# Embedding gate and projection with tokens on partitions, in a one-core decoder layer

## What is computed

```python
gate = jax.nn.sigmoid(_rms_norm(h, lw['norm_ple']) @ lw['w_ple_gate'])   # 1024 x 1024
h = h + gate * (p_l @ lw['w_ple_proj'])                                   # 256 x 1024
```

## Time and profile before

| | us |
|---|---|
| median of 3 executions | 1337.91 (1337.55 to 1339.97) |
| the profiled execution, its own time | 1336.66 |
| its span, first to last instruction | 1334.9 |
| TensorE busy (matmul) | 1252.0 |
| VectorE, ScalarE busy | 329.8, 201.0 |

### The profile page before, as it was taken

How to read it: one execution, slowest core, us unless ns; L and a number is a source line. 1 busy time by engine, 2 the same in 40 slices (tenths; PEclk the granted TensorE clock), 3 DMA queues, 4 the chain that set the end, 5 groups by cost and what they waited for, 6 DMA issues and landing times.

```text
span 1334.9 us, 15918 instructions
## 1 busy us (share of the span) xinstructions
PE 1252.0 (94%) x6170; PEld 618.2 (46%) x6170; DVE 329.8 (25%) x574; ACT 201.0 (15%) x385; POOL 19.9 (1%) x51
## 2 busy tenths in 40 slices
PE   7888798899999999999999999999999999999875
PEld 5768676343434343434434343434344343434354
DVE  7773224112111111121121111111211211111233
ACT  3423403001011010111010101101110101100022
POOL 1010000000000000000000000000000000000000
PEclk9786688899999999999999999999999999998888
DMA  8037203689999999999999999999999999998400
GB/s 254 12 128 303 76 1 135 269 360 366 401 414 405 424 406 423 389 423 408 423 403 398 403 407 423 408 422 405 422 409 423 402 415 419 399 384 368 176 2 32
DMA packets 73262, 438.47 MB, mean 328 GB/s; under 512 B 13617, under 2 KB 16817, under 8 KB 22497
## 3 DMA queue, kind: packets, MB, share of 16 engines
q1 hardware_dynamic: 72736, 437.64, 80.6%
q10 hardware_dynamic: 496, 0.43, 0.1%
HBM read 436.67 MB, written 2.41 MB: 329 GB/s over the span
## 4 chain that ended last, share of the span: by engine, by line
PE 90%; ACT 4%; DVE 3%; issue 2%; ACTq 0%; DVEq 0%
PE ps L922 39%; PE ps L939 18%; PE ps L908 10%; PE ps L878 5%; PE ps L811 2%; PE ps L1051 2%; PE ps L930 2%; PE ps L881 1%; PE ps L603 1%; PE ps L512 1%; PE ps L585 1%; PE ps L543 1%; PE ps L739 1%; PE ps L994 1%; PE ps L948 1%
## 5 line engine op out<-in xcount | busy, mean ns | idle before, releaser
L922 PE MATMUL ps<-ring_up,region 128*64 128x512 f32 x2112 | 461.9, 595 | 2.6 <-issue 1.4
L922 PEld LDWEIGHTS ps<-ring_up,region 128*64 128x64 f32 x2112 | 163.7, 137 | 282.7 <-issue 280.8
L939 PE MATMUL ps<-ring_dn,region 128*64 128x512 f32 x1056 | 246.8, 622 | 12.4 <-issue 11.0
L1825 DVE TENSOR_SCALAR region<-ps 128x512 f32<-128x512 f32 x33 | 22.8, 692 | 711.9 <-PE ps L922 711.9
L939 PEld LDWEIGHTS ps<-ring_dn,region 128*64 128x64 f32 x1056 | 82.7, 142 | 163.4 <-issue 161.2
L908 PE MATMUL ps<-region,n_tok 128*128 128x128 f32 (+1 forms) x768 | 136.7, 309 | 0.0
L908 PEld LDWEIGHTS ps<-region,n_tok 128*128 128x128 f32 (+1 forms) x768 | 105.0, 189 | 41.3 <-issue 12.4
L1304 ACT ACTIVATE region<-region 128x512 f32<-128x512 f32 x33 | 20.8, 629 | 500.3 <-DVE region L1825 500.3
L1316 ACT ACTIVATE region<-ps 64x512 f32<-64x512 f32 x66 | 39.0, 591 | 269.7 <-PE ps L939 269.3
L878 PE MATMUL ps<-region 128*128 128x512 f32 (+1 forms) x136 | 65.9, 607 | 2.6 <-issue 1.3
L922 PE MATMUL ps<-region 128*64 128x512 f32 x264 | 62.7, 592 | 0.0
(11 more groups left out here) (363 smaller groups left out, 788.6 us busy)
## 6 DMA issues: line engine op xcount, KB each, us to landing
ring_up<-in_w_up_dram SPq DMA_DIRECT2D x264, 1024.0 KB, 11.9
ring_dn<-in_w_down_dram SPq DMA_DIRECT2D x132, 1024.0 KB, 7.8
ring_dn<-in_w_out_dram SPq DMA_DIRECT2D x1, 4096.0 KB, 13.3
ring_up<-in_w_ple_gate_dram SPq DMA_DIRECT2D x4, 1024.0 KB, 6.3
ring_up<-in_w_in_dram SPq DMA_DIRECT2D x2, 1536.0 KB, 8.9
ring_up<-in_w_in_dram SPq DMA_DIRECT2D x2, 1024.0 KB, 8.9
x_tok<-in_x_prompt_dram SPq DMA_DIRECT2D x2, 512.0 KB
ring_up<-in_w_glu_dram SPq DMA_DIRECT2D x1, 1024.0 KB, 5.5
```

Source lines behind the costliest of these rows:

```text
L922: m = mm(ps[64 * (q % 2):64 * (q % 2) + 64, q // 2, :], xe[:, k, slots] if k < UP else one_hot, w, start=(k == 0), stop=(k == UP))
L939: m = mm(ps[64 * half:64 * half + 64, O_B, :], act_t[:, f % 4, 64 * (f // 4):64 * (f // 4) + 64], ring_dn[:, f, 512 * half:512 * half + 51 ...
L1825: V.tensor_scalar(g_lim, bank(0), LIMIT, None, ALU.min).then_inc(Z["g_rdy"], 1)
```

## The change

The gate and the projection are computed with tokens on partitions and 512 output columns in a piece: two halves for each of the prompt chunks and one piece for the samples, five in all. The samples' gate goes in four column groups of 256 columns, each on its own 32 partitions of PSUM; their projection goes in two groups of 512. `back` and its transposes are gone, as are the scaling and its place ahead of the transposes for the prompt chunks: the raw rows are turned as soon as the expert shares are in, and the row factor goes into the sigmoid as a scale for each partition. The samples are still scaled first. A chunk's rows are finished, normalised and stored as soon as its pieces are done, the last chunk in two halves. All five pieces of the projection now stand ahead of the counting.

```diff
-PP_BANK = (6, 7, 0, 1, 2, 6, 7, 0)
+PP_BANK = (6, 7, 0, 1, 2)
+PIECES = len(PP_BANK)
+Z_TURN = ((3, 4), (0, 1), (5, 5))
+Z_BANK = (6, 7, 2, 3, 4)
...
# SyncE
-            sp.wait_ge(Z["f_out"], 3)
-            for c in range(2):
-                sp.dma_start(O[0][0, c * P:(c + 1) * P, :], n_tok[:, c]).then_inc(Z["st_y"], 16)
+            sp.wait_ge(Z["f_out"], 1)
+            sp.dma_start(O[0][0, 0:P, :], n_tok[:, 0]).then_inc(Z["st_y"], 16)
+            sp.wait_ge(Z["f_out"], 2)
             sp.dma_start(O[1].rearrange("b l d -> (b l) d"), n_tok[0:NB, 2]).then_inc(Z["st_y"], 16)
+            for half in range(2):
+                at = slice(512 * half, 512 * half + 512)
+                sp.wait_ge(Z["f_out"], 3 + half)
+                sp.dma_start(O[0][0, P:SEQ, at], n_tok[:, 1, at]).then_inc(Z["st_y"], 16)
...
# TensorE, projection (all before the counting; the two late pieces are gone)
+            def embedding():
+                for c in range(2):
+                    for half in range(2):
+                        for k in range(2):
+                            m = mm(bank(PP_BANK[2 * c + half]), p_t[:, k, c * P:(c + 1) * P],
+                                   w_pp[:, k, 512 * half:512 * half + 512], start=(k == 0), stop=(k == 1))
+                        m.then_inc(Z["pp_ps"], 1)
+                for k in range(2):
+                    for half in range(2):
+                        m = mm(ps[64 * half:64 * half + NB, PP_BANK[4], :], p_t[:, k, SEQ:T],
+                               w_pp[:, k, 512 * half:512 * half + 512], start=(k == 0), stop=(k == 1))
+                m.then_inc(Z["pp_ps"], 1)
...
# TensorE, tail
+            def gate_rows(c, half):
+                for k in range(KD):
+                    m = mm(bank(Z_BANK[3 * c + half]), fb[:, k, c * P:(c + 1) * P], w_gate[:, k, 512 * half:512 * half + 512],
+                           start=(k == 0), stop=(k == KD - 1))
+                m.then_inc(Z["gate_ps"], 1)
+            def gate_samples():
+                for k in range(KD):
+                    for q in range(4):
+                        m = mm(ps[32 * q:32 * q + NB, Z_BANK[2], 0:256], fb[:, k, SEQ:T], w_gate[:, k, 256 * q:256 * q + 256],
+                               start=(k == 0), stop=(k == KD - 1))
+                m.then_inc(Z["gate_ps"], 1)
+            pe.wait_ge(Z["cmb_read"], (n_visits + PAIRS) * 4 + 1)
+            turn_tail(0, x_tok)
+            pe.wait_ge(Z["cmb_read"], (n_visits + PAIRS) * 4 + 4)
+            turn_tail(1, x_tok)
+            pe.wait_ge(Z["norm_sb"], 14)
+            pe.wait_ge(ld_gate_w, 64)
+            gate_rows(0, 0)
+            pe.wait_ge(Z["norm_scaled"], 7)
+            turn_tail(2, n_tok)
+            gate_rows(0, 1)
+            pe.wait_ge(Z["norm_sb"], 17)
+            gate_samples()
+            gate_rows(1, 0)
+            gate_rows(1, 1)
...
# ScalarE, tail
+            for n_, c in enumerate((0, 2, 1)):
                 act.wait_ge(Z["cmb_read"], (n_visits + PAIRS) * 4 + (1, 4, 3)[c])
+                row_square(c)
+                row_root(6 + n_ + 1, c)
+            def gate_piece(n_):
+                act.wait_ge(Z["gate_ps"], KM + n_ + 1)
+                c, half = divmod(n_, 3)
+                if n_ == 2:
+                    for q in range(4):
+                        m = f(ple_s[:, 256 * q:256 * q + 256], ps[32 * q:32 * q + NB, Z_BANK[2], 0:256], ACT.Sigmoid)
+                else:
+                    act.wait_ge(Z["z_root"], c + 1)
+                    if n_ > 2:
+                        act.wait_ge(Z["x_gated"], n_ - 2)
+                    m = f(ple_f[half], bank(Z_BANK[n_]), ACT.Sigmoid, scale=stat[:, c, 2:3])
+                m.then_inc(Z["gate_sig"], 1)
+            for n_ in range(3):
+                gate_piece(n_)
+            act.wait_ge(Z["x_gated"], 2)
+            row_square(0)
+            act.wait_ge(Z["x_gated"], 3)
+            row_square(2)
+            row_root(10, 0)
+            row_root(11, 2)
+            gate_piece(3)
+            half_square(0)
+            gate_piece(4)
+            f(stat[:, 0, 3:4], eps, ACT.Sqrt)
+            half_square(1)
+            act.wait_ge(Z["norm_ssq"], 13)
+            act.wait_ge(Z["z_root"], 3)
+            f(stat[:, 1, 1:2], stat[:, 1, 0:1], ACT.Sqrt, scale=1.0 / D, bias=stat[:, 1, 3:4]).then_inc(Z["norm_root"], 1)
...
# VectorE, tail
+            gained(0, 13)
+            row_rate(7, 0).then_inc(Z["z_root"], 1)
+            chain(row_rate(8, 2))
+            V.tensor_scalar(n_tok[0:NB, 2], x_tok[0:NB, 2], stat[0:NB, 2, 2:3], None, ALU.mult
+                            ).then_inc(Z["norm_scaled"], 1)
+            gained(1, 15)
+            row_rate(9, 1).then_inc(Z["z_root"], 1)
+            gained(2, 17)
+            for n_ in range(3):
+                add_piece(n_)
+            chain(row_rate(10, 0))
+            output(0, 1)
+            chain(row_rate(11, 2))
+            output(2, 1)
+            add_piece(3)
+            dve.wait_ge(Z["norm_ssq"], 12)
+            V.scalar_tensor_tensor(stat[:, 1, 3:4], stat[:, 1, 3:4], 1.0 / D, eps, ALU.mult, ALU.add
+                                   ).then_inc(Z["z_root"], 1)
+            add_piece(4)
+            chain(row_rate(12, 1))
+            output(1, 2)
```

More of the change, by code:

```diff
@@ L242, in hybrid_layer @@
         mask = part(3 * NE).rearrange("p (c n) -> p c n", c=3)
-        sg_t = part(2 * T).rearrange("p (a t) -> p a t", a=2)
+        ple_f = [region[:, used_at:used_at + 512] for used_at in (sig_at - 512, sig_at)]
+        ple_s = region[0:NB, sig_at + 512:sig_at + 512 + D]
         sq = proj[:, 0:2]
@@ L841, in _ @@
             pe.wait_ge(Z["pT_sb"], 1)
[L843 to L852, removed]
+            def embedding():
[10 more added lines that the diff above has]
+                m.then_inc(Z["pp_ps"], 1)
+            embedding()
             pe.wait_ge(Z["mask_sb"], 1)
@@ L1020, in _ @@
             combine(PAIRS - 1)
[L1021 to L1031, removed]
@@ L1032, in _ @@
-            pe.wait_ge(Z["norm_sb"], 18)
-            pe.wait_ge(ld_gate_w, 64)
[L1035 to L1055, removed]
+            n_visits = further_visits(pe, visit)
+            def turn_tail(c, rows_):
+                nt = CHUNKS[c][1]
+                for k in range(KD):
+                    at = k % 4 if c < 2 else k
+                    m = tr(ps[:, Z_TURN[c][k // 4], at * nt:(at + 1) * nt], rows_[0:nt, c, k * P:(k + 1) * P],
+                           ident[0:nt, 0:nt])
+                    if c < 2 and k % 4 == 3 or k == KD - 1:
+                        m.then_inc(Z["norm_ps"], 1)
@@ L1342, in _, with row_root @@
[L1342 to L1345, removed]
+            def row_root(n_, c):
+                nt = CHUNKS[c][1]
+                act.wait_ge(Z["norm_ssq"], n_)
+                f(stat[0:nt, c, 1:2], stat[0:nt, c, 0:1], ACT.Sqrt, scale=1.0 / D, bias=eps[0:nt]
+                  ).then_inc(Z["norm_root"], 1)
@@ L1906, in residual @@
[L1906 to L1918, removed]
@@ new lines, in gained @@
+            def gained(c, n_):
+                t0, nt = CHUNKS[c]
+                for half in range(2 if c < 2 else 1):
+                    dve.wait_ge(Z["norm_ps"], n_ + half)
+                    ks = slice(4 * half, 4 * half + 4) if c < 2 else slice(0, KD)
+                    nk = ks.stop - ks.start
+                    V.tensor_tensor(fb[:, ks, t0:t0 + nt],
+                                    ps[:, Z_TURN[c][half], 0:nk * nt].rearrange("p (k n) -> p k n", k=nk),
+                                    col(vecs[:, V_PLE + ks.start:V_PLE + ks.stop], nt), ALU.mult
+                                    ).then_inc(Z["norm_sb"], 1)
@@ new lines, in _, with add_piece @@
+            gained(0, 13)
[6 more added lines that the diff above has]
+            gained(2, 17)
+            def add_piece(n_):
+                c, half = divmod(n_, 3)
+                dve.wait_ge(Z["gate_sig"], KM + n_ + 1)
+                if n_ == 2:
+                    x, s_, p_ = x_tok[0:NB, 2], ple_s, pp_s
+                else:
+                    at = slice(512 * half, 512 * half + 512)
+                    x, s_, p_ = x_tok[:, c, at], ple_f[half], pp_tok[:, c, at]
+                chain(V.tensor_tensor(s_, s_, p_, ALU.mult))
+                V.tensor_tensor(x, x, s_, ALU.add).then_inc(Z["x_gated"], 1)
@@ new lines, in output @@
+            def output(c, pieces):
+                nt, w = CHUNKS[c][1], D // pieces
+                for i in range(pieces):
+                    at = slice(w * i, w * i + w)
+                    V.scalar_tensor_tensor(n_tok[0:nt, c, at], x_tok[0:nt, c, at], stat[0:nt, c, 2:3], final_g[0:nt, at],
+                                           ALU.mult, ALU.mult).then_inc(Z["f_out"], 1)
+            dve.wait_ge(Z["pp_sb"], PIECES)
+            dve.wait_ge(ld_router, 64)
+            for n_ in range(3):
+                add_piece(n_)
```

71 lines of the change are left out of this document (35 added, 36 removed).

## The result

The changed kernel has a median of 1326.7 us (1322.09 to 1329.73, 11 executions) against 1333.52 us for the kernel before over 11 executions (1329.26 to 1339.97). The ratio is 0.9943, 95% interval 0.9925 to 0.996: 7.6 us faster, between 5.3 and 10.0. The forecast was 14.1 faster. The three executions of the kernel before that the prediction started from lay at the upper end of its spread; with more of them its median came down by 4.4 us. The measured time landed inside the predicted range by luck of that start: the same sum from 1333.52 would have said 1319.4, and the gain is about half of the forecast one.

What follows compares the result with a forecast made beforehand. TensorE was taken to bound the span, and a chain of handovers the tail. Gate start -7.9, length +1.8, chain behind -6.6, stores -1.7, projection +0.3 made -14.1 us, so 1323.8 us, range 1321.5 to 1328.5.

Steps and rivals of the forecast that it cites:

- The start of the gate: Tail: turning raw rows lets the gate start at about 1279.7 instead of 1287.59, 7.9 us earlier.
- The gate itself: Gate matmuls: 27.5 us for prompt chunks, 3.9 for samples, 1.0 transposes, 0.3 shape changes; 32.7 together.
- the rival: Samples' gate: eight-column weights do not run four abreast, 13.8 us instead of 3.9, total 1333.7; chance 0.07.
- The end: From last gate matmul to last scaling: 4.94 us, with at most 0.2 of the root's table load showing.
- The store: Last 256 KB store after the last scaling: 3.2 us, kept between 2.5 and 4.9.
- What is hidden: Mid-gate ScalarE work on samples and chunk 0 finishes by 1310.5, before the last piece's matmuls end at 1312.4.
- The cover of 2 us: ScalarE's slack before the last gate matmuls end; if it goes, the excess is paid in full.
- The clock at the gate: Gap before the gate: 16 new transposes should keep TensorE's clock up; rival, clock falls, +2.7 us, chance 0.12.
- the row at 1286: Trace of the kernel before: clock rose from 1286.00 when only transposes had run since 1283.11.
- The projection: Embedding's projection between router and first gather: all pieces ahead of the counting start the gather 0.3 us later.
- the sign of being wrong: Check on the projection: a first gather more than 1.2 us later against the router would refute it.
- The tail: Stretch behind the last expert shares, a chain of handovers: end at 1320.5, 14.4 us earlier.

Runs made afterwards that it cites:

- b2_scaled: Changed kernel plus two idle matmuls ahead of the first gather, with rows scaled before they are turned and no sigmoid scale: 1325.37 us, ratio 0.9922.
- b1_serial: Changed kernel plus two idle matmuls ahead of the first gather, with the samples' gate in one column group instead of four: 1330.91 us, ratio 0.9963.
- a4_before_early: The kernel before with all eight pieces of its projection ahead of the counting, old layout and tail kept: 1342.49 us, ratio 1.0065.
- c1_before_fill: The kernel before with three idle matmuls each behind the up projection of the first expert and of each further visit: 1334.09 us, ratio 0.9984.
- a2_late: Changed kernel with the last prompt piece and the samples' piece of the projection behind the counting again: 1325.6 us, ratio 0.9925.
- a1_again: The changed kernel measured once more, unaltered: 1326.81 us, ratio 0.9949 to the kernel before.

## Why the prediction was right and wrong

*The start of the gate.* Forecast 2.7 us after the last share, measured 2.5. Right; the reason holds too, with a clock gain on top that b2_scaled brought out.

*The gate itself.* Forecast 32.7 us, measured from 1286.82 to 1319.12, 32.3. The nearest row chosen for the samples carried over to eight-column weights: 3.57 us against 3.9. b1_serial gave the rival's price, 13.83 against 13.8, and showed that it doesn't apply.

*The end.* Forecast 4.94 us, measured 1324.01 - 1319.12 = 4.9. The table load is on the chain above, from 1319.85, and hides under VectorE: the addition ends at 1321.28 and the square of the half starts at 1321.31, so less than the 0.2 that was allowed shows.

*The store.* Forecast 3.2, measured 2.5, at the low bound. The 256 KB transfer it was sized by was a load, and on another queue.

*What is hidden.* ScalarE reached piece 3 at 1313.55, 1.4 us after its matmuls ended (1.5 was forecast), and its half square was over 2.1 us before the last matmul. The cover of 2 us was right.

*The clock at the gate.* It stayed up, as the row at 1286 let expect:

```profile
1285.00:1287.00 2.00, 1.60 (x13) 1.14 (x11) 1.93 (x5) 1.96 (x6) 0.00 (x0) 1.00 0.02 4
```

This row alone says little against the rule of the page "TensorE: Matmul & The Clock Gate" of the Trainium skill, section "Part 4: PE-mode transpose", that transpose mode doesn't count: the gate began 2.5 us after the last share. But where TensorE was idle behind the last share the clock fell 1.7 to 2.5 us after it (the kernel before, a4_before_early, c1_before_fill and b2_scaled), and in eight profiles with 16 transposes there it never fell. Against the rule stands, too, that the clock rose while only transposes ran, at 1286 in the kernel before and in the microsecond from 1294.00 in a4_before_early. c1_before_fill shows that such a stream doesn't always do it. So the forecast was right here, with a firmer "transposes lift the clock" than the runs bear out.

*The projection.* This is the step that failed, with its bounds. It was put at +0.3 us, with the words "bounds -0.5 to +1.2, as the clock falls there or not". The times of the parts were near: the counting began 2.8 us later (2.35 was forecast) and the gather 1.1 (0.3), or 0.9 against the router. So the sign of being wrong that was named, a gather more than 1.2 later, did not show: it watched the gather's start and not its length. The bound on the clock was wrong. I took it from a gather that was cold for its first microseconds only, and took for granted that the clock would come back within it. It did not in 14.6 us of gather, and the up projection behind ran its first 5 us at the lower clock too. The gather alone cost 5.6 us, 14.62 against 9.06 in the timeline of before. This was a rival without a place in my list, though the pieces moved away had stood exactly in this wait. I counted them as 2.99 us of cost and not for what they did to the clock: it fell while they ran, but it was back before the gather was two microseconds old.

*The numbers.* 1323.8 was forecast and 1326.7 measured, in the range, but with a baseline 4.4 us lower. The tail gave more than forecast, 15.7, and 0.7 of the excess of 1.3 is the store. The stretch ahead of it took back 7.3 in the profile, most of it in the first gather and the up projection behind it, whose cure alone was worth 6.7.

## What to carry to other kernels

When dense matmuls are moved away from before a wait, ask what TensorE does in the microseconds they leave, and what runs behind it: if that is a stretch of short matmuls like this gather, price it at the lower clock for its whole length. A few idle matmuls into a free bank test this in one run, and can stay. Dense work that is free to move can stand in such a wait instead of where it is first ready: moving it out of there cost the kernel before 8.6 us (a4_before_early). But moving two pieces back in the changed kernel won nothing that is clear of the noise (a2_late), so test the place and don't take it as given.

## What the runs showed that was not expected

A gather's 128-column records took 0.18 us each at full clock and 0.30 us at half (14.62 / 48). Streams of the same gather run at the full clock throughout the loop (8.51 us each), yet in the changed kernel, in a1_again and in a4_before_early the clock, once down, did not rise again while the same stream ran: 14.62, 14.21 and 15.03 us. In the kernel before it rose within this stream, but behind 3 us of dense pieces. Three dense matmuls in a wait of 2.85 us, on the other hand, kept it.

Four groups of eight-column weights gave 3.9 times the speed of one.
